# First-layer queries and keys as one 512-column group with weights moving, turned by VectorE; bias lines turned round; last product re-ordered

## Chip, cores and metric

The kernel runs on one core of one Trainium2 chip. The metric is the device time of one execution in microseconds, the median of three runs.

## What is computed

Two layers of a transformer on 256 tokens of width 2048, all in f32, and behind them a third layer with a convolution branch and windowed attention. The first layer, cut to what matters here:

```python
h = rmsnorm(x, attn_norm[0])
p = h @ even_w_in[0]                    # 2048 x 6144
qa, ka, va, qb, kb, vb = split(p)       # 1024 columns each
oa = chunked_relpos_attention(qa, ka, va, a_rel_bias)     # 8 heads of 128: branch A
ob = diff_attention(qb, kb, vb, t5_b, b_lambda, b_subln)  # 4 heads of 2 x 128: branch B
x = x + concatenate([oa, ob]) @ even_w_out[0]
x = x + (silu(h2 @ w_gate) * (h2 @ w_up)) @ w_down
```

The bias of A and B depends only on the distance of query and key. The second layer attends over selected tokens with latent keys and values, and has the same kind of output product and feed-forward part. The third layer ends in the product with `w_out_2`, a residual sum and a layer norm.

## The kernel before

Every weight is streamed once from HBM in units of 512 KB: SP issues a unit's DMA into `raw` (four slots), ScalarE rounds it to fp32r (`hi`, line 197), VectorE forms the rest (`lo`, line 203) into `ws` (four slots), and TensorE multiplies high and low parts of weights and activations. A unit's slot in `ws` is written again for the unit four further on, so `hi` of unit u + 4 waits for TensorE to be done with unit u (`s_mm`), and `lo` waits for `hi`; the DMA four units ahead again waits for `lo`.

Units are grouped (`Seg`): a group accumulates in two PSUM banks, and groups alternate between banks 0, 1 and 2, 3. There are two forms of multiplication. In `mul_T` (lines 227 to 230) the weights are stationary and the activations `hs` move, so the result comes with its columns in the partitions: a group of 256 columns has four units, and it is what scores need. In `mul_W` (line 251) activations are stationary and 512 weight columns move, twelve matmuls a unit, eight units a group; the result has tokens in the partitions. Before, phase A (`gA`) has ten groups, `QKVQKQKVQK`, where Q and K are of the first form and V of the second; phase B (`gBs`) has `QKVQKQKQKV`. Each phase has 48 units. A group of the first form is emptied by ScalarE (`crossing`, line 377) and VectorE (`scaled_drain`, lines 384 to 391, which writes the queries back to front in blocks), a V group by VectorE (line 1074).

The attention of a head pair is put between the units by hooks. TensorE's hook j of a group runs behind its unit j. `group_side` gives ScalarE and VectorE the hooks j behind `hi` or `lo` of unit j + 4, and an "early" hook stands ahead of it. The steps of a pair: scores `S_` (TensorE, lines 824, 825), `max_` (VectorE, line 839), `exps` (ScalarE, line 850), `soft` (VectorE, line 860, for B lines 927 to 935), the transposes `T_` (TensorE, line 867), `pt_` (ScalarE, line 878), the product with the values `V_` (TensorE, lines 887, 888), `out_hi`, `out_lo`; in B besides the norm of the output: `b_sq`, `b_st`, `b_a`, `rstd_act`, `b_on`, `b_hi`, `b_lo`. GpSimd (`stage`) brings the bias of a pair from DRAM, where two tables of lines (`lineA`, `lineB`) were written, each line read with a shift of one per partition, and copies it to `biasM` (line 1093).

`residual` is the output product with the residual sum. VectorE turns its result in 32x32 blocks (`turn_block`, line 585: 16 stream transposes a group) for the next product. `conv_*`, `gate_silu` and `late_out` finish the third layer's branches inside the last product (`so_run`), whose tables `so_act` and `so_dve` give ScalarE's and VectorE's work by unit.

Of the kernel before, what the change touches and what calls it, by code (L numbers as in the profile page):

```python
# [68 lines left out]
def build(nc, a):  # L69
# [228 lines left out]
    gA = Seg(1, [4, 4, 8, 4, 4, 4, 4, 8, 4, 4], [0, 2] * 5)  # L298
    gBs = Seg(1, [4, 4, 8, 4, 4, 4, 4, 4, 4, 8], [0, 2] * 5)
# [1809 lines left out]
```

## Time and profile before

| | |
|---|---|
| median of three runs | 2485.19 us (2485.16 to 2485.97) |
| profiled execution | 2484.79 us |
| its span, first to last instruction | 2483.0 us |
| TensorE busy | 2459.4 us (99%), mean granted clock 0.997 |
| VectorE busy | 1694.9 us (68%) |
| ScalarE busy | 1195.4 us (48%) |
| GpSimd busy | 52.8 us (2%) |
| DMA | 463.17 MB, 187 GB/s |

In the rows PE is TensorE's matmuls, PEld its weight loads, DVE VectorE, ACT ScalarE, POOL GpSimd. L251 is line 251 of the kernel. Times are us from the start of the span. A matmul's shown duration reaches into the next one, so the distance of two starts is what one costs. An idle time in brackets names the instruction that ended it.

### The profile page before, as it was taken

How to read it: one execution, taken by the hardware profiler on the slowest of the kernel's cores; microseconds unless marked ns; L12 is line 12 of the kernel's file. 1: busy time of each engine (PE TensorE's matmuls, PEld its weight loads, DVE VectorE, ACT ScalarE, POOL GpSimd, SP SyncE). 2: the span in 40 equal slices, each digit the busy share in tenths (PEclk: the TensorE clock that was granted, in tenths of full speed). 3: DMA queues.
4: the chain of work that ended last, by engine and by line, in shares of the span. 5: the costliest groups of instructions: out<-in, count | busy, mean ns of one | idle time of the engine just before them, and what ended most of it. 6: DMA issues, size and time to landing. Idle time of an engine off the chain costs nothing.

```text
span 2483.0 us, 32501 instructions
## 1 busy us (share of the span) xinstructions
PE 2459.4 (99%) x11622; PEld 2053.0 (83%) x11622; DVE 1694.9 (68%) x2538; ACT 1195.4 (48%) x1570; POOL 52.8 (2%) x72
## 2 busy tenths in 40 slices
PE   9999999999999999999999999999999999999997
PEld 8888888888888888888888888888888888888776
DVE  6556676666666666567867666666666656888985
ACT  5444455444444444445554544444444444546773
POOL 1000000000000000000220000000000000100000
PEclk9999999999999999999999999999999999999998
DMA  7555556666666655557545666666665555765453
GB/s 235 177 179 174 175 172 196 194 191 191 196 191 193 194 195 194 192 168 216 165 144 169 195 194 190 192 196 192 194 193 195 192 193 193 223 184 162 146 192 131
DMA packets 283278, 463.17 MB, mean 187 GB/s; under 512 B 17343, under 2 KB 99441, under 8 KB 282666
## 3 DMA queue, kind: packets, MB, share of 16 engines
q1 hardware_dynamic: 280768, 453.63, 59.5%
q0 software_dynamic: 1792, 8.11, 1.0%
q8 instruction: 63, 1.03, 0.2%
q14 instruction: 37, 0.30, 0.0%
q10 hardware_dynamic: 618, 0.09, 0.0%
HBM read 459.63 MB, written 2.14 MB: 186 GB/s over the span
## 4 chain that ended last, share of the span: by engine, by line
PE 95%; DVE 3%; ACT 1%; issue 1%; DMA 0%; DVEq 0%; ACTq 0%
PE PG L251 78%; PE PG L228 8%; PE PG L227 4%; DVE ws L203 1%; PE PS L824 1%; ACT ws L197 1%; PE PS L867 1%; PE PO L887 0%; PE PG L1280 0%; PE PG L240 0%; PE PO L1289 0%; DVE cacc L1505 0%; PE PS L825 0%; PE PG L230 0%; PE PO L888 0%
## 5 line engine op out<-in xcount | busy, mean ns | idle before, releaser
L203 DVE TENSOR_TENSOR ws<-raw,ws 128x1024 fp32r<-128x1024 f32 x860 | 1055.9, 1229 | 705.9 <-ACT ws L197 699.7
L197 ACT ACTIVATE ws<-raw 128x1024 fp32r<-128x1024 f32 x860 | 909.2, 1059 | 1073.6 <-PE PG L251 924.0
L251 PE MATMUL PG<-ws,hs 128*128 128x512 f32 x5568 | 1275.3, 390 | 0.3 <-DVE ws L203 0.3
L251 PEld LDWEIGHTS PG<-ws,hs 128*128 128x128 f32 x5568 | 1042.1, 188 | 216.6 <-issue 0.4
L251 PE MATMUL PG<-ws,fs 128*128 128x512 f32 x2112 | 479.0, 389 | 0.0
L251 PEld LDWEIGHTS PG<-ws,fs 128*128 128x128 f32 x2112 | 396.4, 188 | 82.3
L228 PE MATMUL PG<-hs,ws 128*128 128x512 f32 x880 | 308.3, 394 | 0.0
L251 PE MATMUL PG<-ws,os 128*128 128x512 f32 x1152 | 265.5, 391 | 2.7 <-DVE ws L203 2.7
L251 PEld LDWEIGHTS PG<-ws,os 128*128 128x128 f32 x1152 | 215.3, 188 | 48.6 <-DVE ws L203 4.2
L227 PE MATMUL PG<-hs,ws 128*128 128x256 f32 x825 | 235.1, 285 | 0.1
L228 PEld LDWEIGHTS PG<-hs,ws 128*128 128x128 f32 x880 | 163.7, 188 | 34.6 <-DVEq L1325 0.3
L585 DVE STREAM_TRANSPOSE turnb<-qst 32x256 f32<-32x256 f32 x352 | 153.4, 436 | 7.2
L227 PEld LDWEIGHTS PG<-hs,ws 128*128 128x128 f32 x825 | 155.7, 189 | 1.9 <-issue 0.4
L1505 DVE SCALAR_TENSOR_TENSOR cacc<-hc,convw,cacc 128x256 f32<-128x256 f32 x232 | 97.9, 478 | 0.0
L585 DVE STREAM_TRANSPOSE turnb<-x 32x256 f32<-32x256 f32 x192 | 83.6, 436 | 3.5
L850 ACT ACTIVATE ts<-ts,small 128x256 f32<-128x256 f32 x96 | 42.4, 443 | 25.4 <-DVE small L842 25.2
L790 ACT ACTIVATE cross<-PG,small 128x512 f32<-128x512 f32 x44 | 27.8, 685 | 33.2 <-PE PG L251 33.2
L803 DVE SCALAR_TENSOR_TENSOR qst<-PG,small,cross 128x512 f32<-128x512 f32 x44 | 31.0, 747 | 10.5 <-PE PG L251 10.5
L377 ACT ACTIVATE cross<-PG 128x512 f32<-128x512 f32 (+1 forms) x28 | 16.4, 587 | 39.8 <-PE PG L228 39.8
L384 DVE TENSOR_TENSOR cross<-PG,cross 128x512 f32<-128x512 f32 (+1 forms) x28 | 19.0, 679 | 18.5 <-ACT cross L377 18.4
L767 ACT ACTIVATE fs<-turnb 128x1024 f32 (+1 forms) x22 | 23.3, 1061 | 15.2 <-DVE turnb L585 15.2
L554 ACT ACTIVATE cross<-x 128x512 f32<-128x512 f32 x40 | 25.3, 632 | 11.2 <-DVE x L738 9.2
(287 smaller groups left out, 912.7 us busy)
## 6 DMA issues: line engine op xcount, KB each, us to landing
raw<-in_w_gate SPq DMA_DIRECT2D x176, 512.0 KB, 4.0
raw<-in_w_up SPq DMA_DIRECT2D x176, 512.0 KB, 4.3
raw<-in_w_down SPq DMA_DIRECT2D x176, 512.0 KB, 3.6
raw<-in_even_w_in SPq DMA_DIRECT2D x96, 512.0 KB, 4.0
raw<-in_w_in SPq DMA_DIRECT2D x52, 512.0 KB, 3.7
raw<-in_odd_w_in SPq DMA_DIRECT2D x44, 512.0 KB, 3.7
raw<-in_even_w_out SPq DMA_DIRECT2D x32, 512.0 KB, 4.3
raw<-in_odd_w_out SPq DMA_DIRECT2D x32, 512.0 KB, 3.6
```

The source lines that it names most:

```text
L197: e.activation(ws[j % RING][:, :, 0, :], raw[:, j % RING], ACT.Copy).then_inc(s_hi, 1)
L203: e.tensor_tensor(w[:, :, 1, :], raw[:, j % RING], w[:, :, 0, :].bitcast(F32), ALU.subtract).then_inc(s_lo, 1)
L227: e.matmul(PG[:, bank + c, 0:S], wl, rhs[:, k0 + kk, 0, :], start=False, stop=False)
L228: ins = e.matmul(PG[:, bank + c, :], wh, both, start=st, stop=end)
L251: ins = e.matmul(out[:, b, :], x_, w[:, kk, :, h, :], start=first and kk == 0 and n == 0, stop=last and kk == 1 and n == 2)
L554: e.activation(junk, xr[:, b, 512 * g:512 * (g + 1)], ACT.Square, accum_out=ss[:, b, g:g + 1]).then_inc(sem(p + "sq"), 1)
L585: return e.transpose(blocks_out, blocks_in)
L790: ins = e.activation(sil[:, b], gates[:, b, :], ACT.Silu, scale=rnT[:, b:b + 1])
L803: ins = e.scalar_tensor_tensor(nat_f[:, b], ups[:, b, :], rnT[:, b:b + 1], sil[:, b], ALU.mult, ALU.mult)
L824: e.matmul(PS[:, h, 0:S], q(h)[:, P:S], k(h), start=True, stop=True)
L850: e.activation(ts[:, h, src], ts[:, h, src], ACT.Exp, bias=nmx[:, n:n + 1], accum_out=sm[:, n:n + 1]).then_inc(sem(p + "e"), 1)
L1505: e.scalar_tensor_tensor(dst, hc[:, n, c:c + S], convw[:, n, c:c + 1], dst, ALU.mult, ALU.add).then_inc(sem("cv"), 1)
```

## The change

- **Queries and keys.** A group X now holds 256 query and the 256 key columns that belong to them, as a unit of two k-tiles by 512 columns (`pair_cols`, two DMAs of 256 KB), multiplied by `mul_W`. The phases are `XVXXVX` and `XVXXXV`, six groups of eight units each. ScalarE empties every group, scaled by a column, for X into `natqk`; `turn_pair` turns it on VectorE into `qk`, 16 stream transposes a pair. `pair_steps` hooks these by four behind units 0 to 3 of the group after X, the scores behind unit 4, the maxima early at unit 5, the softmax behind unit 6, transposes and values behind units 0 and 2 of the group after that. The spreading of the norm's factor over a tile and the drains on VectorE fall away in the first layer.
- **Start.** DMAs of x's last two quarters come behind four weight units; the transposes of the second quarter come behind unit 0; part of the dummy transposes fall away.
- **Bias lines.** The lines are written in the other direction, so queries and the scores' transposes are no longer turned round; instead GpSimd reads the bias back to front. The index scores and masks of the second layer follow.
- **Odd output product.** Transposes and values of the last head pair come one unit later.
- **Last product.** ScalarE's and VectorE's work at units 3 to 6 is ordered anew.

Its core:

```diff
+    natqk = at("natqk", [P, 2, 2, 512], F32, o1 + 24576)
+    qk = at("qk", [P, 2, 4, S], F32, o1 + 32768)
...
-        halved = min((u - gCv.ub) // RING + 1, gCv.U // RING) if isinstance(u, int) and u >= gCv.ub else 0
+        halved = sum(v % RING == j % RING and v <= (u if isinstance(u, int) else gEO.ub) for v in in_two)
...
-    gA = Seg(1, [4, 4, 8, 4, 4, 4, 4, 8, 4, 4], [0, 2] * 5)
-    gBs = Seg(1, [4, 4, 8, 4, 4, 4, 4, 4, 4, 8], [0, 2] * 5)
+    gA = Seg(1, [8] * 6, [0, 2] * 3)
+    gBs = Seg(1, [8] * 6, [0, 2] * 3)
...
+    order_of = {"A": "XVXXVX", "B": "XVXXXV"}
+    in_two = [sg.ub + 8 * g + j for sg, p in ((gA, "A"), (gBs, "B")) for g, kind in enumerate(order_of[p]) if kind == "X" for j in range(8)]
+    in_two += [gCv.ub + j for j in range(gCv.U)]
...
+    def pair_cols(W, j, c0):
+
+        return [W.rearrange("(t p) n -> p t n", p=P)[:, 2 * j:2 * j + 2, c:c + UC] for c in (c0, c0 + 1024)]
...
     def setup_sp(e):
         for c in range(4):
-            x_load(e, c)
-            load(e, gA, 0, c, cols(a["even_w_in"][0], c, 0))
+            if c < 2:
+                x_load(e, c)
+            load(e, gA, 0, c, pair_cols(a["even_w_in"][0], c, 0), 2)
+        x_load(e, 2)
+        x_load(e, 3)
...
-        src = bass.AP(tensor=lines.tensor, offset=h0 * LINE, ap=[[1, P], [LINE, n], [1, S]])
+        src = bass.AP(tensor=lines.tensor, offset=h0 * LINE + 1, ap=[[1, P], [LINE, n], [1, S]])
...
         lo(e, 0, 0)
         slice_lo(e, 0)
         lo(e, 1, 1)
+        lo(e, 2, 2)
         slice_lo(e, 1)
-        lo(e, 2, 2)
-        slice_lo(e, 2)
         lo(e, 3, 3)
-        slice_lo(e, 3)
         lines_first(e)
...
+    def back_to_front(t):
+
+        n = t.shape[2]
+        v = t[:, :, n - 1:n]
+        return bass.AP(tensor=v.tensor, offset=v.offset, ap=[list(v.ap[0]), list(v.ap[1]), [-1, n]])
...
         slice_hi(e, 0)
         hi(e, 1, 1)
-        slice_hi(e, 1)
         hi(e, 2, 2)
         squares(e, "n0", 0)
-        slice_hi(e, 2)
+        slice_hi(e, 1)
         hi(e, 3, 3)
-        slice_hi(e, 3)
-        squares(e, "n0", 1)
...
         keep_busy(e, 7)
         x_pe(e, 0)
-        keep_busy(e, 8)
-        x_pe(e, 1)
         keep_busy(e, 10)
...
-    def flipped(e, p, j, heads=slice(0, 2), turned=True):
+    def flipped(e, p, j, heads=slice(0, 2)):
 
         w(e, p + "T", j + 1)
         w(e, p + "O", j)
-        src = PS[:, heads, 0:384]
-        if turned:
-            v, n = PS[:, heads.start:heads.start + 1, P - 1:P], heads.stop - heads.start
-            src = bass.AP(tensor=v.tensor, offset=v.offset, ap=[list(v.ap[0]), [512, n], [P, 3], [-1, P]])
-            e.activation(pT[:, heads, :].rearrange("p h (b s) -> p h b s", s=P), src, ACT.Copy).then_inc(sem(p + "pT"), 1)
-            return
-        e.activation(pT[:, heads, :], src, ACT.Copy).then_inc(sem(p + "pT"), 1)
+        e.activation(pT[:, heads, :], PS[:, heads, 0:384], ACT.Copy).then_inc(sem(p + "pT"), 1)
...
+        def root_scale(e):
+            e.tensor_scalar(column, rnT, SCALE ** 0.5, None, ALU.mult).then_inc(sem("rq"), 1)
+
+        def number(pp, j):
+            return 4 * (pp == "B") + j
+
+        def turn_pair(e, pp, j, part):
+
+            x = number(pp, j)
+            if part[0] == 0:
+                g = [n for n, kind in enumerate(order_of[pp]) if kind == "X"][j]
+                e.wait_ge(s_drain, (gA if pp == "A" else gBs).group(0, g) + 3)
+            for n in part:
+                r, c = 32 * (n // 4), 32 * (n % 4)
+                blocks_in = natqk[r:r + 32, x % 2].rearrange("p b (t c) -> p b t c", c=P)[:, :, :, c:c + 32]
+                blocks_out = qk[c:c + 32, x % 2].rearrange("p t (b s) -> p b t s", s=P)[:, :, :, r:r + 32]
+                ins = e.transpose(blocks_out, blocks_in)
+            if part[-1] == 15:
+                ins.then_inc(sem("qkT"), 1)
 
         def S_(e, pp, j):
-            sg = gA if pp == "A" else gBs
-            scores(e, pp, j, lambda h: qst[:, 0, h, :], lambda h: kst[:, h, :],
-                   lambda: e.wait_ge(s_drain, sg.group(0, at_k[pp][j]) + 3))
+            x = number(pp, j)
+            scores(e, pp, j, lambda h, b: qk[:, x % 2, h, b * P:(b + 1) * P], lambda h: qk[:, x % 2, 2 + h, :], lambda: e.wait_ge(sem("qkT"), x + 1))
...
+                "pe": {0: {0: lambda e: x_pe(e, 1), 1: lambda e: (x_pe(e, 2), tables_pe(e)), 3: lambda e: x_pe(e, 3)}, 1: {1: lam_pe}},
+                "act": {0: {0: lambda e: squares(e, "n0", 1), 1: lambda e: slice_hi(e, 2), 2: lambda e: squares(e, "n0", 2), 3: lambda e: slice_hi(e, 3),
+                            4: lambda e: squares(e, "n0", 3), 5: lambda e: norm_act(e, "n0")}, 1: {2: lam_act}},
+                "dve": {0: {1: lambda e: slice_lo(e, 2), 2: lines_second, 3: lambda e: slice_lo(e, 3), 4: lambda e: norm_first(e, "n0"), 5: lambda e: (norm_second(e, "n0"), root_scale(e))},
+                        1: {3: lam_dve}}}[name].items()}
...
+        def put(at, g, u, d, f, early=False):
+
+            g, u = g + (u + d) // 8, (u + d) % 8
+            u = ("early", u) if early else u
+            at[g, u] = (lambda f0=at[g, u]: (f0(), f())) if (g, u) in at else f
+
+        def pair_steps(name, e, at, pp, j, g):
+
+            if name == "pe":
+                put(at, g, 4, 0, lambda: S_(e, pp, j))
+                if number(pp, j) < 7:
+                    put(at, g, 4, 4, lambda: T_(e, pp, j))
+                if number(pp, j) < 6:
+                    put(at, g, 4, 6, lambda: V_(e, pp, j))
+            elif name == "act":
+                put(at, g, 4, 1, lambda: exps(e, pp, j))
+                if number(pp, j) < 7:
+                    put(at, g, 4, 4, lambda: pt_(e, pp, j))
+                if pp == "A":
+                    put(at, g, 4, 7, lambda: out_hi(e, pp, j, 2 * j))
+            else:
+                for n in range(4):
+                    put(at, g, n, 0, lambda n=n: turn_pair(e, pp, j, range(4 * n, 4 * n + 4)))
+                put(at, g, 4, 1, lambda: max_(e, pp, j), early=True)
+                put(at, g, 4, 2, lambda: soft(e, pp, j))
+                if pp == "A":
+                    put(at, g, 4, 7, lambda: out_lo(e, pp, j, 2 * j))
+
+        def norm_steps(name, e, at, j, g):
+
+            if name == "pe":
+                put(at, g, 4, 0, lambda: b_st(e, j))
+            elif name == "act":
+                put(at, g, 2, 0, lambda: b_sq(e, j))
+                put(at, g, 5, 0, lambda: rstd_act(e, "B", j))
+                put(at, g, 7, 0, lambda: b_hi(e, j))
+            else:
+                put(at, g, 5, 0, lambda: b_a(e, j), early=True)
+                put(at, g, 6, 0, lambda: b_on(e, j))
+                put(at, g, 7, 0, lambda: b_lo(e, j))
...
+                for g, v in start_hooks(name, e).items():
+                    at.update({(g, j): f for j, f in v.items()})
+                for j, g in enumerate((1, 3, 4)):
+                    pair_steps(name, e, at, "A", j, g)
...
+            pair_steps(name, e, at, "A", 3, 0)
+            norm_steps(name, e, at, 0, 2)
+            norm_steps(name, e, at, 1, 4)
+            for j, g in enumerate((1, 3, 4, 5)):
+                pair_steps(name, e, at, "B", j, g)
...
+                        group_pe(e, seg, 0, g, W_mul(hs), hk, (lambda j: w(e, "n0lo", 2 * j + 2)) if first and not is_b else None)
                     elif name == "act":
-                        def cross_over(_):
-                            if kind != "V":
-                                if not is_b:
-                                    w(e, "n0sq", 8)
-                                crossing(e, seg, 0, g)
-                        group_side(e, seg, 0, g, hi, cross_over, hk)
+                        def drain(_):
+                            e.wait_ge(s_mm, seg.end(0, g) + RING)
+                            pairs_seen = number(p, order_of[p][:g].count("X"))
+                            if kind == "X":
+                                e.wait_ge(sem("rq"), 1)
+                                w(e, "qkT", pairs_seen - 1)
+                            for b in (0, 1):
+                                out = natqk[:, pairs_seen % 2, b, :] if kind == "X" else vab[:, order_of[p][:g].count("V"), b, :]
+                                ins = e.activation(out, PG[:, seg.banks[g] + b, :], ACT.Copy, scale=(column if kind == "X" else rnT)[:, b:b + 1])
+                            ins.then_inc(s_drain, 1)
+                        group_side(e, seg, 0, g, hi, drain, hk)
...
-                e.tensor_copy(biasM[:, 0:n, 0:S], biasE[:, h:h + n, :]).then_inc(sem(p + "bm"), 1)
+                e.tensor_copy(biasM[:, 0:n, 0:S], back_to_front(biasE[:, h:h + n, :])).then_inc(sem(p + "bm"), 1)
...
-             {0: lambda e: (c_S(e, 7, 1), c_V(e, 6, 0)), 2: lambda e: flips(e, "C", 7), 3: lambda e: c_V(e, 7, 1)},
-             {0: lambda e: out_hi(e, "C", 6, 12), ("early", 1): lambda e: exps(e, "C", 7), 2: lambda e: flipped(e, "C", 7), 3: lambda e: out_hi(e, "C", 7, 14)},
-             {0: lambda e: c_max(e, 7), 1: lambda e: out_lo(e, "C", 6, 12), ("early", 2): lambda e: norms(e, "C", 7), ("early", 4): lambda e: out_lo(e, "C", 7, 14)})
+             {0: lambda e: (c_S(e, 7, 1), c_V(e, 6, 0)), 3: lambda e: flips(e, "C", 7), 4: lambda e: c_V(e, 7, 1)},
+             {0: lambda e: out_hi(e, "C", 6, 12), ("early", 1): lambda e: exps(e, "C", 7), 3: lambda e: flipped(e, "C", 7), 4: lambda e: out_hi(e, "C", 7, 14)},
+             {0: lambda e: c_max(e, 7), 1: lambda e: out_lo(e, "C", 6, 12), ("early", 2): lambda e: norms(e, "C", 7), ("early", 5): lambda e: out_lo(e, "C", 7, 14)})
...
         rstd_act(e, "L")
         e.preload_act_table(ACT.Silu)
-        conv_silu(e, 0)
-        conv_silu(e, 1)
...
-              4: lambda e: (conv_hi(e, 0), conv_hi(e, 1), late_out(e, 9, 1), conv_silu(e, 2)),
-              5: lambda e: (gate_silu(e, slice(4, 8), 20), conv_silu(e, 3)), 6: lambda e: conv_hi(e, 2), 7: lambda e: conv_hi(e, 3),
+              4: lambda e: (conv_silu(e, 0), conv_hi(e, 0), conv_silu(e, 1)),
+              5: lambda e: (conv_hi(e, 1), late_out(e, 9, 1), gate_silu(e, slice(4, 8), 20), conv_silu(e, 2)),
+              6: lambda e: (conv_silu(e, 3), conv_hi(e, 2)), 7: lambda e: conv_hi(e, 3),
...
-    so_dve = {0: first_dve, 2: lambda e: (spread_dve(e), conv_scale(e, 0), conv_scale(e, 1)),
-              3: lambda e: (centre_conv(e, 1), conv_gate(e, 0), conv_gate(e, 1), conv_lo(e, 0)),
-              4: lambda e: (conv_lo(e, 1), conv_scale(e, 2), conv_scale(e, 3)),
+    so_dve = {0: first_dve, 2: lambda e: (spread_dve(e), conv_scale(e, 0)),
+              3: lambda e: (conv_gate(e, 0), conv_scale(e, 1), conv_lo(e, 0)), 4: lambda e: conv_gate(e, 1),
+              5: lambda e: (conv_lo(e, 1), centre_conv(e, 1), conv_scale(e, 2), conv_scale(e, 3)),
               6: lambda e: (conv_gate(e, 2), conv_gate(e, 3), conv_lo(e, 2)), 7: lambda e: conv_lo(e, 3)}
```

## Rows read from the trace of the kernel before

**Rows 1.** The page's fourth part: shares of the chain that ended last, by engine.

```profile
PE 95%; DVE 3%; ACT 1%; issue 1%; DMA 0%; DVEq 0%; ACTq 0%
```

**Rows 2.** Waits of PE, whole span: us in total, times, longest.

```profile
PE PG L251 <- DVE ws L203: 3.0, 4, 1.6
```

**Rows 3.** Timeline of PE: start, us, line, operation, count, idle before and its releaser.

```profile
37.22 3.00 PE L251 MATMUL PG<-ws,hs 128*128 128x512 f32 x12 [0.30 <-DVE ws L203]
...
1302.08 5.70 PE L251 MATMUL PG<-ws,os 128*128 128x512 f32 x24
...
1309.33 0.88 PE L867 MATMUL PS<-ident,ts 128*128 128x128 f32 x6 [1.55 <-DVE ts L860]
...
2386.52 11.17 PE L251 MATMUL PG<-ws,os 128*128 128x512 f32 x48
...
2402.93 5.90 PE L251 MATMUL PG<-ws,os 128*128 128x512 f32 x24 [1.58 <-DVE ws L203]
...
2409.29 15.98 PE L251 MATMUL PG<-ws,os 128*128 128x512 f32 x69 [0.46 <-DVE ws L203]
```

**Rows 4.** Chain that ended last, in order of time: start, us, what.

```profile
9.45 0.87 PE PG L613 x8
...
33.60 0.45 PE PO L706 x2
...
73.68 0.46 PE PG L228 x2
...
84.97 0.46 PE PG L228 x2
...
116.23 0.43 PE PS L824 x2
...
117.53 10.94 PE PG L251 x48
...
128.47 0.66 PE PS L867 x6
...
220.71 0.46 PE PG L228 x2
...
231.82 0.46 PE PG L228 x2
```

**Rows 5.** Timeline of DVE in phase A, a low part behind a free slot.

```profile
121.50 1.23 DVE L203 TENSOR_TENSOR ws<-raw,ws 128x1024 fp32r<-128x1024 f32 x1 [1.53 <-ACT ws L197]
```

**Rows 6.** Timeline of DVE in the even output product: low parts and turning quarters.

```profile
335.63 1.23 DVE L203 TENSOR_TENSOR ws<-raw,ws 128x1024 fp32r<-128x1024 f32 x1 [1.50 <-ACT ws L197]
...
336.77 1.78 DVE L585 STREAM_TRANSPOSE turnb<-x 32x256 f32<-32x256 f32 x4
...
338.56 1.23 DVE L203 TENSOR_TENSOR ws<-raw,ws 128x1024 fp32r<-128x1024 f32 x1
...
339.82 1.78 DVE L585 STREAM_TRANSPOSE turnb<-x 32x256 f32<-32x256 f32 x4
```

**Rows 7.** Timeline of DVE in phase B: norm, output, softmax and what follows each.

```profile
226.06 0.42 DVE L655 TENSOR_TENSOR nt<-na,ny 128x256 f32<-128x256 f32 x1
...
228.37 1.22 DVE L203 TENSOR_TENSOR ws<-raw,ws 128x1024 fp32r<-128x1024 f32 x1
...
231.61 0.88 DVE L989 SCALAR_TENSOR_TENSOR os<-qst,small,os 128x256 fp32r<-128x256 f32 x2
...
244.06 0.17 DVE L927 RECIPROCAL small<-small 128x4 f32<-128x4 f32 x1
...
245.72 0.68 DVE L384 TENSOR_TENSOR cross<-PG,cross 128x512 f32<-128x512 f32 x1
```

**Rows 8.** Timeline of DVE in the last product: two scalings of 128x512.

```profile
2391.58 1.29 DVE L1879 TENSOR_TENSOR cacc<-cacc,ny 128x512 f32<-128x512 f32 x2
```

**Rows 9.** Timeline of POOL: first copy of the bias.

```profile
35.93 1.62 POOL L1093 COPY biasM<-biasE 128x512 f32<-128x512 f32 x1
```

**Rows 10.** Windows: stretch, length, each engine's busy us (count), clock, DMA share, GB/s.

```profile
2400.00:2405.00 5.00, 3.42 (x15) 2.50 (x15) 1.78 (x3) 4.50 (x7) 0.00 (x0) 1.00 0.41 138
```

More of the change, by code:

```diff
@@ L215, in load, with mul_T @@
         e.dma_start(dst, src).then_inc(s_raw[j % RING], 16)
-    def mul_T(e, bank, j, k0, rhs, first, last, tiles=(0, 1), ready=lambda kk: None):
+    def mul_T(e, bank, j, k0, rhs, first, last, tiles=(0, 1)):
         w = ws[j % RING]
         for kk in range(UK):
-            ready(kk)
             for c in tiles:
@@ L377, in crossing, with scaled_drain @@
         e.activation(cross[:, q // 2, 0:m], PG[:, q:q + m, S:2 * S], ACT.Copy).then_inc(s_cross, 1)
-    def scaled_drain(e, seg, i, k, dst, crossed, n, scale=1.0, turned=None):
+    def scaled_drain(e, seg, i, k, dst, crossed, n, scale=1.0):
         m, q = dst.shape[1], seg.banks[k]
@@ L385, in scaled_drain @@
         e.wait_ge(sem("summed"), n + 1)
-        if turned is None:
-            return e.scalar_tensor_tensor(dst, c, scale, bc(rn, m), ALU.mult, ALU.mult)
-        if turned:
-            e.scalar_tensor_tensor(dst[0:turned], c[0:turned], scale, bc(rn, m)[0:turned], ALU.mult, ALU.mult)
-        t = slice(turned, P)
-        return e.scalar_tensor_tensor(backward(dst[t]), blocks(c[t]), scale, blocks(bc(rn, m)[t]), ALU.mult, ALU.mult)
+        return e.scalar_tensor_tensor(dst, c, scale, bc(rn, m), ALU.mult, ALU.mult)
     QT = D // 4
@@ L1020, in out @@
-            def out(pp, j, g, u):
-                put(e, at, {"pe": {}, "act": {(g, u): lambda: out_hi(e, pp, j, 2 * j)}, "dve": {(g, u): lambda: out_lo(e, pp, j, 2 * j)}}[name])
-            if not is_b:
-                for k, v in start_hooks(name, e).items():
-                    put(e, at, {(k, j): f for j, f in v.items()})
-                broad("A", 0, 2)
-                out("A", 0, 3, 2)
-                narrow("A", 1, 5)
-                out("A", 1, 6, 3)
-                broad("A", 2, 7)
-                out("A", 2, 8, 2)
-                return at
@@ L1052, in f @@
                     hk = {j: f_ for (g_, j), f_ in at.items() if g_ == g}
-                    n = order_of[p][:g].count("Q") + order_of[p][:g].count("K")
                     if name == "pe":
-                        mul = W_mul(hs) if kind == "V" else T_mul(hs)
-                        if first and not is_b:
-                            mul = lambda e, bank, jj, j, f_, l_: mul_T(e, bank, jj, UK * j, hs, f_, l_, ready=lambda kk: w(e, "n0lo", 4 * j + kk + 1))
-                        group_pe(e, seg, 0, g, mul, hk)
+                        group_pe(e, seg, 0, g, W_mul(hs), hk, (lambda j: w(e, "n0lo", 2 * j + 2)) if first and not is_b else None)
@@ L1100, in weights @@
                 n = order_of[p][:g].count(kind)
-                for j in range(seg.groups[g]):
+                for j in range(8):
                     if kind == "V":
-                        load(e, seg, 0, seg.first(g) + j, wide_cols(W, j, c0 + 2048 + 2 * UC * n), 1)
-                    elif is_b or g:
-                        load(e, seg, 0, seg.first(g) + j, cols(W, j, c0 + 1024 * (kind == "K") + UC * n))
+                        load(e, seg, 0, 8 * g + j, wide_cols(W, j, c0 + 2048 + 2 * UC * n), 1)
+                    elif is_b or g or j > 3:
+                        load(e, seg, 0, 8 * g + j, pair_cols(W, j, c0 + UC * n), 2)
         phase(sp=weights, pe=run("pe"), act=run("act"), dve=run("dve"), pool=stage)
@@ L1335, in c_S @@
     def c_S(e, j, par):
-        scores(e, "C", j, lambda h: qst[:, par, h, :], lambda h: kC[:, bass.ds(2 * j + h, 1), :][:, 0, :],
+        scores(e, "C", j, lambda h, b: qst[:, par, h, b * P:(b + 1) * P], lambda h: kC[:, bass.ds(2 * j + h, 1), :][:, 0, :],
                lambda: e.wait_ge(s_drain, gQ.gb + j + 3))
@@ L1362, in c_pool @@
         prepare(1, 1)
-        def body(i, *_):
-            prepare(2 * i, 0)
-            prepare(2 * i + 1, 1)
-        with e.Fori(1, 4) as i:
-            body(i)
+        for j in range(2, 8):
+            prepare(j, j % 2)
     def c_hooks(name, e, j, par):
@@ L1794, in act @@
                     n, j = n0 + 2 * g + half, 4 * half
-                    hk["early", j] = lambda n=n: n == 0 or flipped(e, "D", n - 1, turned=False)
+                    hk["early", j] = lambda n=n: n == 0 or flipped(e, "D", n - 1)
                     hk[j] = lambda j=j: start_at(e, name_of, g, j)
@@ L1900, in first_act @@
     def first_act(e):
-        flipped(e, "D", 7, turned=False)
+        flipped(e, "D", 7)
         gate_silu(e, slice(12, 16), 16)
```

86 lines of the change are left out of this document (19 added, 67 removed).

## The prediction

> **What bounds the kernel now.** I read the chain that ended last first: TensorE is 95% of it [rows 1], so in nearly every stage only what delays or shortens TensorE's own queue counts. Then the waits of that queue [rows 2]: behind the set-up it waits for VectorE's low parts four times, 3.0 us in all. Its timeline [rows 3] places them: 0.30 us at 37.22, 1.55 at 1309.33 in the odd output product (for the softmax), the rest from 2398 to 2409 in the last product. In the first layer's projections, 37 to 305 us, it waits for nothing. VectorE and ScalarE have slack there, and what the change gives them costs time only where TensorE comes to wait for it.
>
> **Measures for the sums.** A unit is one 512 KB weight tile. In the form with weights moving (12 matmuls of 512 columns) four units take 10.94 us, 2.735 each (at 117.53) [rows 4]. In the form with weights stationary a group of four units takes 11.29 us (73.68 to 84.97) or 11.11 (220.71 to 231.82), mean 2.80 a unit [rows 4]. A block of scores takes 1.30 us (116.23 to 117.53), the six transposes of the weights 0.66 [rows 4].
>
> **Queries and keys in one group.** After the first eight units, phases A and B have 24 + 32 = 56 units of the stationary form. They turn into the moving form: 56 x (2.80 - 2.735) = 3.6 us less; by the two rows 2.4 to 4.9. The scores, transposes and value products are as many as before.
>
> **The turning, which I think decides.** The result of such a group has the sequence in its partitions and must be turned: 16 stream transposes a pair, eight pairs. `pair_steps` hooks four of them behind VectorE's low parts of units 0, 1, 2 and 3 of the next group, and puts the scores into TensorE's queue behind unit 4, with a wait for the sixteenth. The added wait stands in TensorE's queue, so units 5 to 7 and all that follows wait with it. How late is the sixteenth? A low part's slot comes free only when TensorE is done with the unit. The unit that ends at 117.53 + 2.735 = 120.265 [rows 4] has its low part start at 121.50 [rows 5]: 1.235 us behind the unit's end. VectorE then goes on to the next thing 1.14 us later, four transposes of just this shape hold it 1.79, and from a low part queued directly behind them to the next four are 1.26 [rows 6]. So, from the end of unit 0: first four done at 1.235 + 1.14 + 1.79 = 4.17. Each further quarter takes 1.26 + 1.79 = 3.05, more than TensorE's 2.735, so VectorE is not held up by units any more: 7.22, 10.27, 13.32. There the scores can start. TensorE comes to them at 4 x 2.735 = 10.94. Wait: 2.38 us. Were VectorE caught up before the last quarter, it would still be 4.17 - 2.735 = 1.43, since the last quarter is hooked only one unit ahead of its user.
>
> Pair by pair: A0, A1, A3 and B1 are of this clean kind: 4 x 2.38 = 9.5 (A0 has three small lambda instructions ahead of its last quarter, which I leave to the range). In A2's and B0's group TensorE also does the last pair's transposes (0.66) and values (1.30, as the scores) between units 0 and 4, which delays TensorE by 1.96; VectorE, held to unit 3 again, then does `out_lo` (0.65, one 128x512 instruction as in [rows 8]) and the last quarter. Same count: 2.13 each, 4.3. At B2 transposes of one head (0.33), values and the sum of squares (0.86, four matmuls as the two of 0.43 at 116.23) precede the scores, and the wait shrinks to 0.6. At B3 VectorE comes with a debt: in B2's group unit 6 has `b_on` (2.31 us, 226.06 to 228.37) and `soft` (1.66, 244.06 to 245.72), unit 7 `b_lo` (0.88) [rows 7]. The softmax is ready 0.9 us after TensorE asks for it, and the turning starts at 16.36 instead of 2.38 on a clock in which its unit 0 ends at 12.25; the same steps end 2.8 us behind TensorE. Together 9.5 + 4.3 + 0.6 + 0.9 + 2.8 = 18.1 us. Bounds: 11.5 (each of eight at 1.43) and 25 (each as B3, with A0's three and more debt).
>
> The Trainium skill speaks against this move: VectorE: DVE Perf Modes, The three transpose paths and Rules for kernel authors, send a 128x128 transpose to TensorE where PSUM may hold it, since VectorE turns 32x32 blocks only. Its figure for VectorE's 128x128, 311 ns for bf16, would make an estimate of 0.62 us for a quarter here, and the waits would shrink to about 0.3 us each; no run shows that pace, the rows above show 1.79.
>
> **Drains.** ScalarE empties both kinds of group now (two 128x512 reads ahead of one high part, 1.3 us if they take what VectorE's two take [rows 8]), VectorE none. ScalarE's high part of that unit comes later by that, the low part too, and its user is three units, 8.2 us, behind: nothing while that cover stands; gone, it would be 1.3 us a group. Two DMAs for one on SP's queue go the same way: their data is asked for four units ahead. Both at nothing.
>
> **Set-up.** The first group's eight units get 8 x (11.11/4 - 2.735) = 0.3 us shorter, the spread product (0.45, at 33.60) goes, and the 0.30 wait at 37.22 [rows 3, 4]; against that the transposes of x's second quarter (0.87, at 9.45) [rows 4], until now done while TensorE had to wait anyway, come behind unit 0, and unit 0 needs a second tile's low part, 0.4 later (two of that kind take 0.88 [rows 7]). Sum 0.2; I take 0, range -0.5 to +1.5. Dummy transposes fall away ahead of unit 0, so TensorE is idle there for a while.
>
> **Bias lines turned round.** GpSimd copies the bias back to front now. The first copy ends at 37.55 [rows 9] and is needed behind unit 4 of the second group, at about 37.2 + 5 x 2.735 = 51; later ones have a whole pair. Even at twice its 1.62 us it is hidden. Without that cover it would hold the maxima, and through them the softmax. The scores, transposed reads and selection in the odd layer only lose or exchange a negative stride; the plain and the turned forms of the drain bound that at nothing. Zero, range 0 to 1.
>
> **Odd output product.** The last transposes move from behind unit 2 to behind unit 3. From 1302.08 to 1309.33 two units take 7.25 where 5.47 are work [rows 3]: 1.8 us go, as the weights were 1.55 late and a unit is 2.735. The values follow one unit later and their low part is needed two units after; nothing is late next. Range 1.5 to 1.8.
>
> **Last product.** Unit 4 starts at 2386.52, unit 11 at 2409.29 [rows 3]: 22.77 us for 19.15 of work, 3.6 lost. The new order lets the low part of unit 8 go ahead of most of the gating. Worked out from 2391.58 [rows 8] in queue order, with ScalarE's work at the lengths it has in this stage (a pair of Silus 1.05, a 128x512 copy 0.6, a high part 1.0): scale 0 and low part 7 to 2393.3, gate 0 behind the first Silu to 2394.1, scale 1, first output part, then low part 8 done at 2396.6, before TensorE wants it (2386.52 + 10.94 = 2397.46). Low part 9 ends at 2398.4. But high part 10 stands behind the third Silu, which waits for the centring and scaling on VectorE: low part 10 ends at 2404.2, against 2402.93: 1.3 late. Low part 11, behind `conv_hi` 2, ends at 2407.7 against 2407.0: 0.75. Unit 11 starts at 2407.75: 1.5 us gained, range 0 to 3.6.
>
> **Sum** against the profiled execution, 2484.79 us (span 2483.0 and 1.8 around it): 2484.8 - 3.6 + 18.1 + 0 - 1.8 - 1.5 = 2496.0. The median of the runs shown is 0.4 above that execution: 2496.4 us. The forecast's own range: all terms at their friendly ends 2485.2 - 4.9 + 11.5 - 0.5 - 1.8 - 3.6 = 2485.9, at the others 2485.2 - 2.4 + 25 + 1.5 + 1 - 1.5 - 0 = 2508.8; since they hardly all fall together, 2488 to 2504.
>
> **Rivals.** *No wait at the scores.* If the turning is through before unit 4 ends, by a faster transpose or because I misplace a hook, what is left is 2485.2 - 3.6 - 1.8 - 1.5 = 2478.3, faster. It decides from the point where a quarter takes under about 0.35 us from the last low part on; every row at 1.79 speaks against it, that all four quarters are named ahead of unit 4 speaks for it. Chance 0.11. The figure of the Trainium skill's page VectorE: DVE Perf Modes would leave 8 x 0.26 = 2.1 us of waits, 2480.4, of which I hold 0.01 of that chance. *The waits are there, but short* (1.5 or less each, VectorE never in debt): 8 x 1.5 or less on 2478.3 gives 2480 to 2490. The rows' 3.05 against 2.735 speaks against it. Chance 0.10. *The clock.* Nine waits of 2.4 us could let TensorE's clock fall from 2.4 to 1.2 GHz. The row of 2400 to 2405 holds the 1.58 us gap and shows a granted clock of 1.00 [rows 10]; no longer gap inside the work is there to judge by. A fall that lasts one unit costs 2.7 us: with each of nine, 25 us, about 2521. Chance 0.05. The Trainium skill's page TensorE: Matmul & The Clock Gate, HAM oscillation, has idle gaps between bursts put a kernel back to the low clock each time. *ScalarE or the streams late*: the drain ahead of the high part and the debts add up past the 8.2 us of cover at some groups, 1.3 us each, 12 groups: up to 2512. Chance 0.04.
>
> **Chances.** Forecast 0.70. A run tells about 0.2%, 5 us, from no change: faster (below 2480.2) is the first rival, 0.11; same takes the short waits and a little of the forecast's low end, 0.12; slower 0.77. The range leaves out the first rival and the clock: 2484 to 2505.
>
> **What would show it.** In the profile after: TensorE's waits list, at its top, the scores' line held by VectorE's transposes, eight times, 1.5 to 3 us each, the shortest at B2; phase A + B about 15 us longer though matmuls of the large form take 0.228 us apart throughout; the wait at 1309 gone; two waits of about 1 us in place of three in the last product. Wrong it is if the scores start directly behind unit 4, if a quarter of the turning takes other than 1.8 us, or if the granted clock leaves 1.00.

## The result and the profile after

| | before | after |
|---|---|---|
| median | 2485.58 us (2485.16 to 2486.67, 4 runs) | 2507.16 us (2506.87 to 2507.44, 4 runs) |
| ratio | | 1.0086, 95% interval 1.0069 to 1.0104 |
| profiled execution, its span | 2484.79, 2483.0 us | 2507.44, 2505.6 us |

The change makes the kernel 21.6 us slower. The forecast was 11.2 us slower (2496.4, range 2484 to 2505): the right sign, about half the size, and the result lies outside the range.

First the waits of TensorE in the kernel after (engine, line, what it waited for: us in total, times, longest). They answer to [rows 2].

```profile
PE PS L815 <- DVE qk L910: 17.7, 8, 2.8
...
PE PG L252 <- DVE ws L205: 1.8, 2, 1.4
PE PS L858 <- DVE ts L938: 1.7, 1, 1.7
...
PE PG L252 <- DVE hs L561: 0.8, 1, 0.8
```

The scores (L815) wait eight times for the turning (L910), where [rows 2] had no wait of this kind. The transposes of B2 (L858) wait once for the softmax. A0 to A3 are the head pairs of branch A, B0 to B3 those of branch B. TensorE's timeline of after gives each wait its place (start, us, what, idle before and its releaser), in the order A0, A1, A2, A3, B0, B1, B2 (scores, then transposes), B3:

```profile
53.50 0.70 PE L815 MATMUL PS<-qk 128*128 128x256 f32 x2 [2.54 <-DVE qk L910]
...
104.75 0.70 PE L815 MATMUL PS<-qk 128*128 128x256 f32 x2 [2.46 <-DVE qk L910]
...
133.94 0.70 PE L815 MATMUL PS<-qk 128*128 128x256 f32 x2 [2.18 <-DVE qk L910]
...
183.58 0.70 PE L815 MATMUL PS<-qk 128*128 128x256 f32 x2 [2.46 <-DVE qk L910]
...
212.80 0.70 PE L815 MATMUL PS<-qk 128*128 128x256 f32 x2 [2.17 <-DVE qk L910]
...
263.32 1.22 PE L815 MATMUL PS<-qk 128*128 128x256 f32 x2 [2.76 <-DVE qk L910]
...
291.43 0.70 PE L815 MATMUL PS<-qk 128*128 128x256 f32 x2 [0.71 <-DVE qk L910]
...
305.65 0.55 PE L858 MATMUL PS<-ident,ts 128*128 128x128 f32 x3 [1.73 <-DVE ts L938]
...
319.57 0.70 PE L815 MATMUL PS<-qk 128*128 128x256 f32 x2 [2.46 <-DVE qk L910]
```

Together 19.5 us. In the row of 263.32 the same two matmuls take 1.22 us and not 0.70: they run at half the clock. Windows of after show the granted clock, as a share of 2.4 GHz (stretch, length, busy us of PE, PEld, DVE, ACT, POOL with counts, then the clock, DMA share and GB/s). The reader is to look at the number behind POOL:

```profile
54.00:58.00 4.00, 4.00 (x14) 3.29 (x14) 2.12 (x11) 0.00 (x0) 1.14 (x2) 0.58 0.46 143
104.00:110.00 6.00, 5.25 (x18) 4.39 (x19) 3.32 (x13) 0.00 (x0) 1.26 (x2) 0.72 0.58 177
134.00:138.00 4.00, 4.00 (x20) 3.44 (x21) 2.56 (x11) 0.00 (x0) 0.95 (x2) 1.00 0.45 152
184.00:188.00 4.00, 4.00 (x15) 3.27 (x14) 2.22 (x11) 0.00 (x0) 0.60 (x3) 0.57 0.62 199
212.00:216.00 4.00, 3.20 (x16) 2.80 (x17) 3.37 (x13) 0.00 (x0) 0.15 (x1) 1.00 0.50 156
262.00:268.00 6.00, 4.68 (x16) 3.98 (x17) 3.88 (x14) 0.00 (x0) 0.22 (x1) 0.72 0.55 175
306.00:310.00 4.00, 4.00 (x20) 3.30 (x19) 3.96 (x8) 1.44 (x2) 0.00 (x0) 1.00 0.43 135
318.00:326.00 8.00, 6.43 (x23) 5.33 (x24) 4.11 (x15) 0.68 (x2) 0.00 (x0) 0.79 0.44 140
```

Behind A0, A1, A3, B1 and B3 TensorE's clock went from 2.4 to 1.2 GHz and came back; this is called a fall below. Behind A2, B0 and the wait of B2's transposes it stayed. What a fall takes is the length of a window times one minus its clock: 4 x 0.42, 6 x 0.28, 4 x 0.43, 6 x 0.28 and 8 x 0.21, about 1.7 us each, 8.5 together. The row of before that answers is [rows 10], with 1.00.

Phases A and B go from 267.8 us (37.22 to 305.01) to 293.8 (36.96 to 330.78): 26.0 more. The forecast for the moving form was 3.6 less; the listed waits are 19.5 and the clock 8.5, which leaves 1.6. Most of that is in the waits themselves, since the list counts idle time from the end that is shown, and a matmul's shown duration reaches past what it costs. For A1:

```profile
99.64 2.65 PE L252 MATMUL PG<-ws,hs 128*128 128x512 f32 x11
104.75 0.70 PE L815 MATMUL PS<-qk 128*128 128x256 f32 x2 [2.46 <-DVE qk L910]
```

Eleven matmuls at 0.228 end at 102.15 and not at 102.29, so the wait is 2.60 and not 2.46. Counted like this the nine waits are 20.9 us together, and 25.8 of the 26.0 have a place, if the 3.6 are right.

### The profile page after: what moved, and what is told of

Read it like the earlier page. It is cut to its first block, busy times and chain, and to the rows that moved or that the text cites. A ratio compares the mean times of both kernels' runs of the same rounds, so it can differ in the third digit from the quotient of the medians.

```text
span 2505.6 us, 32089 instructions
## 1 busy us (share of the span) xinstructions
PE 2464.0 (98%) x11356; PEld 2045.3 (82%) x11356; DVE 1723.3 (69%) x2623; ACT 1202.1 (48%) x1578; POOL 51.7 (2%) x72
## 4 chain that ended last, share of the span: by engine, by line
PE 81%; DVE 4%; ACT 1%; issue 1%; DVEq 0%; ACTq 0%
PE PG L252 74%; PE PG L229 3%; PE PG L228 1%; DVE ws L205 1%; PE PG L241 0%; ACT ws L199 0%; DVE cacc L1508 0%; PE PG L1286 0%; PE PS L858 0%; PE PO L872 0%; PE PS L815 0%; DVE pT L1179 0%; PE PO L1295 0%; DVE x L2059 0%; ACT ts L1709 0%
## 5 line engine op out<-in xcount | busy, mean ns | idle before, releaser
L252 PE MATMUL PG<-ws,hs 128*128 128x512 f32 x6336 | 1459.8, 391 | 0.8 <-DVE hs L561 0.8
L252 PEld LDWEIGHTS PG<-ws,hs 128*128 128x128 f32 x6336 | 1189.4, 188 | 247.8 <-issue 1.0
L229 PE MATMUL PG<-hs,ws 128*128 128x512 f32 x368 | 129.0, 394 | 0.0
L228 PE MATMUL PG<-hs,ws 128*128 128x256 f32 x345 | 98.9, 287 | 0.2 <-DVE hs L561 0.2
L229 PEld LDWEIGHTS PG<-hs,ws 128*128 128x128 f32 x368 | 68.4, 188 | 14.2 <-DVEq L1331 0.3
L228 PEld LDWEIGHTS PG<-hs,ws 128*128 128x128 f32 x345 | 65.1, 189 | 1.2 <-issue 0.4
L910 DVE STREAM_TRANSPOSE qk<-natqk 32x256 f32<-32x256 f32 x128 | 55.8, 436 | 2.1
L547 ACT ACTIVATE cross<-x 128x512 f32<-128x512 f32 x40 | 25.3, 632 | 11.2 <-DVE x L729 9.2
L815 PE MATMUL PS<-qk 128*128 128x256 f32 x32 | 12.0, 462 | 17.7 <-DVE qk L910 17.7
```

Of the source, the lines that this page charges most:

```text
L228: e.matmul(PG[:, bank + c, 0:S], wl, rhs[:, k0 + kk, 0, :], start=False, stop=False)
L229: ins = e.matmul(PG[:, bank + c, :], wh, both, start=st, stop=end)
L252: ins = e.matmul(out[:, b, :], x_, w[:, kk, :, h, :], start=first and kk == 0 and n == 0, stop=last and kk == 1 and n == 2)
L547: e.activation(junk, xr[:, b, 512 * g:512 * (g + 1)], ACT.Square, accum_out=ss[:, b, g:g + 1]).then_inc(sem(p + "sq"), 1)
L910: ins = e.transpose(blocks_out, blocks_in)
```

## Experiments

Two theories. *Theory 1*: the order of the hooks makes the waits, since VectorE's quarter takes longer than TensorE's unit, and some waits let the clock fall. *Theory 2*: something else in the new form (ScalarE's drains, two DMAs a tile, the set-up, VectorE's debts) costs the missing 10.8 us.

**The scores one unit later.** A pair's whole chain moves, from S_ to out_lo, the norm's steps too; the turning stays.

```
-                put(at, g, 4, 0, lambda: S_(e, pp, j))
+                put(at, g, 5, 0, lambda: S_(e, pp, j))
...
-                put(at, g, 6, 0, lambda: b_on(e, j))
+                put(at, g, 6, 1, lambda: b_on(e, j))
```

> The kernel after, with the scores and all that hangs on them (maxima, exponentials, softmax, transposes, values, norms) one unit later, behind unit 5 of a group instead of unit 4; the turning stays where it is. Theory 1 (the order of hooks makes the waits, and the waits make the clock fall): VectorE is through with the turning 13.3 us behind unit 0, TensorE comes at 13.7, so at least six of the eight waits go, B3 may keep up to 1.5; no granted clock under 1.00 between 37 and 305 us; phases A and B take 264 to 268 us instead of 293.9, the kernel 2507.2 - 29 + (0 to 3) = 2478 to 2481. Theory 2 (something else in the new form costs most of it: ScalarE's drains, two DMAs a tile, the form itself): only the listed waits of 17.7 us go, 2489 or more, and other waits or longer units appear.

Measured: 2487.96 us, ratio 1.0009 (0.9999 to 1.0018). 19.2 us go, not 26 to 29. Seven of the eight waits at the scores are gone. Three waits are left in TensorE's timeline:

```profile
247.41 0.70 PE L815 MATMUL PS<-qk 128*128 128x256 f32 x2 [2.34 <-DVE qk L910]
...
288.48 0.90 PE L858 MATMUL PS<-ident,ts 128*128 128x128 f32 x3 [2.87 <-DVE ts L938]
...
334.74 5.46 PE L252 MATMUL PG<-ws,os 128*128 128x512 f32 x23 [1.28 <-DVE os L992]
```

and the clock falls behind the second, for longer than in any wait of after (10 us at 0.66, 3.4 us lost):

```profile
286.00:296.00 10.00, 7.52 (x22) 6.08 (x23) 9.11 (x21) 3.40 (x5) 0.00 (x0) 0.66 0.44 143
```

2478.3 (the sum without waits) + 2.34 + 2.87 + 1.28 + 3.4 = 2488.2. The expectation of 2478 to 2481 missed, I think, because I moved the norm's steps as well: b_lo came ahead of B1's first quarter, and b_on ahead of B2's softmax; the next run tests it. That speaks for theory 1, but with several things moved at once it isn't a proof.

**The same, with the norm's steps left in their place.** The edit is shown against the kernel just before. Of the norm only the squares stay one unit later; the softmax now goes ahead of the norm's scaling, and in the output product the last pair's norm is scaled a unit earlier than in the kernel just before.

```
-                put(at, g, 6, 1, lambda: b_on(e, j))
+                put(at, g, 6, 0, lambda: b_on(e, j))
...
-            norm_steps(name, e, at, 0, 2)
-            norm_steps(name, e, at, 1, 4)
             for j, g in enumerate((1, 3, 4, 5)):
                 pair_steps(name, e, at, "B", j, g)
+            norm_steps(name, e, at, 0, 2)
+            norm_steps(name, e, at, 1, 4)
```

> As the kernel with the scores a unit later (2487.96), but the steps of the norm (reciprocal root, scaling, low part of heads 8 on) go back to the units where the kernel after has them, only the squares stay one later, the softmax goes ahead of them at unit 7, and the last norm in the output product is scaled a unit earlier. In that kernel's trace these late steps are what holds the rest: 2.34 us at B1's scores, 2.87 at B2's transposes, with a fall of the clock behind it, 1.28 in the output product. Theory 1 (what is left above 2478.3 is these three and the fall): 2.6 + 3.1 + 1.7 + 1.5 = 8.9 us go, 2479 to 2481, faster than before (2485.6) by about 0.2%. Theory 2 (the moving form or the set-up cost something not seen as a wait): 2483 or more, with clock 1.00 and no waits.

Measured: 2479.87 us (2479.57 to 2481.90, 11 runs), ratio 0.9979 (0.9970 to 0.9988), faster than both kernels. One wait is left at the scores, B3's, and the window of phases A and B has a full clock:

```profile
PE PS L815 <- DVE qk L910: 1.3, 1, 1.3
```

```profile
36.00:305.00 269.00, 267.65 (x1224) 221.68 (x1223) 191.16 (x358) 130.93 (x199) 9.51 (x22) 1.00 0.57 180
```

2478.3 + 1.3 = 2479.6 against 2479.87. With waits and falls gone, everything else in the change comes to the sum that the prediction had put down, so theory 2 falls: nothing near 10 us is left for it. That the two agree to 0.3 us is in part luck. The interval of the ratio is about 2 us to each side, and in this trace the second group starts at 36.65, 0.6 us earlier than before where 0 was put down, while phases A and B (to 303.07) are 1.4 us shorter, or 2.9 without the wait, where 3.6 was put down.

**The waits filled with work.** Dummy transposes ahead of the scores in five pairs; the scores start when they did.

```
         x = number(pp, j)
+        w(e, pp + "pT", j)
+        for _ in range((22, 22, 0, 22, 0, 22, 0, 22)[x]):
+            e.transpose(PS[:, 0, 384:512], ident[:], ident[:])
```

> The kernel after, with 22 dummy transposes (0.11 us each, 2.4 us) in TensorE's queue ahead of the wait at the scores of A0, A1, A3, B1 and B3, the five behind which the granted clock was 0.67 to 0.83. TensorE comes to the scores at the same time, but has worked until then. Theory 1 (these five waits let the clock fall, 1.7 us lost each): clock 1.00 in 53 to 60, 104 to 110, 183 to 190, 263 to 268, 320 to 330; scores of these pairs 0.70 us for the first two matmuls and not 1.22; the kernel 2507.2 - 8.3 = about 2499. Theory 2 (the clock is no part of the missing 10 us, VectorE's debts are): no change, 2507, or up to 2 us more where a dummy ends behind the sixteenth transpose.

Measured: 2500.07 us, ratio 1.0056 (1.0040 to 1.0073): 7.1 us less for work that nobody reads. The five falls are gone, as expected. A new one came at B0, whose wait is what it was (2.18 us):

```profile
206.00:212.00 6.00, 4.52 (x15) 3.76 (x16) 4.02 (x15) 0.45 (x1) 0.85 (x2) 0.72 0.58 178
```

Five falls less and one more are four: 1.8 us each by the medians, against 1.7 from the windows; in the two traces the stretch from behind the second group's second unit to the output product is 6.2 us shorter, 1.6 each. TensorE comes to the scores when it did and only isn't idle until then, so this shows the clock's share directly.

**Shorter idle times.** The same edit with 4 and with 8 dummies.

> As the one before, but with only four dummy transposes (0.44 us) ahead of each of the same five waits: the idle time is 2.46 - 0.44 = about 2.0 us in each, shorter than the 2.17 and 2.18 behind which the clock stayed. Theory 1 with a bound between 2.18 and 2.46 us of idle time: clock 1.00 throughout, about 2499. Theory 1 with a cost that grows with the length of the wait: a small part of the 8.3 us, 2505 to 2507. Theory 2 (not the gap's length but the pair decides): clock falls as before, 2507.

Measured: 2503.59 us, ratio 1.0070 (1.0053 to 1.0087). None of the three expectations is met. The waits that were 2.46 to 2.76 are now 2.00 to 2.32; the clock still falls in A0, A1 and A3, and doesn't in B1 and B3. Timeline and window of A3, then of B1:

```profile
183.97 0.81 PE L815 MATMUL PS<-qk 128*128 128x256 f32 x2 [2.00 <-DVE qk L910]
...
263.71 0.70 PE L815 MATMUL PS<-qk 128*128 128x256 f32 x2 [2.32 <-DVE qk L910]
```

```profile
184.00:188.00 4.00, 4.00 (x13) 3.38 (x14) 2.43 (x11) 0.00 (x0) 0.00 (x0) 0.57 0.64 215
...
262.00:268.00 6.00, 4.29 (x21) 3.69 (x22) 4.25 (x15) 0.11 (x1) 0.88 (x2) 1.00 0.56 175
```

A wait of 2.00 let it fall and one of 2.32 did not. So in the one execution traced, length alone doesn't decide between 2.0 and 2.5 us.

> The kernel after with eight dummy transposes (0.88 us) ahead of the scores of A0, A1, A3, B1 and B3. With four, waits of 2.00 to 2.10 us still let the clock fall in A0, A1 and A3, but not 2.32 and 2.02 in B1 and B3. Now the waits are about 1.6 us. If the idle time's length decides together with something else, no clock falls at this length, 2500 as with 22. If the place alone decides (A0, A1, A3 fall whatever the length, so long as there is a wait), the clock falls at these three and the time is 2503 to 2505.

Measured: 2501.43 us, ratio 1.0066 (1.0051 to 1.0081). A0, A1, A3, B1 and B3 now wait 1.57 to 1.87 us and none falls. The place alone is refuted. One fall is left, at B0 again, behind a wait of the length that left the clock alone in after (2.17):

```profile
207.88 1.07 PE L815 MATMUL PS<-qk 128*128 128x256 f32 x2 [2.18 <-DVE qk L910]
```

**The same waits at other moments.** Twelve dummy transposes behind unit 6 of the first group were to make every wait come 1.3 us later.

```
-                "pe": {0: {0: lambda e: x_pe(e, 1), 1: lambda e: (x_pe(e, 2), tables_pe(e)), 3: lambda e: x_pe(e, 3)}, 1: {1: lam_pe}},
+                "pe": {0: {0: lambda e: x_pe(e, 1), 1: lambda e: (x_pe(e, 2), tables_pe(e)), 3: lambda e: x_pe(e, 3), 6: lambda e: keep_busy(e, 12)}, 1: {1: lam_pe}},
```

> The kernel after with 12 dummy transposes (1.3 us of work) behind unit 6 of the first group: every wait behind it is as long as before and comes 1.3 us later. If the place of a wait within some rhythm of the chip decides which of them lets the clock fall, other pairs than A0, A1, A3, B1 and B3 show a granted clock under 1.00. If the length decides (2.46 and more fall, 2.18 and less not), the same five. The time: 2507.2 + 1.3 = 2508.5 for the same five, up to 1.7 us less or more for each fall that goes or comes.

Measured: 2506.81 us, ratio 1.0084 (1.0069 to 1.0100). The waits are as long as before to 0.01 us, the falls are not the same: A1, A3, B0 and B1. Windows of A0, B0 and B3 in this kernel, then the scores of A1 and B0:

```profile
54.00:58.00 4.00, 3.04 (x16) 2.63 (x17) 3.37 (x14) 0.00 (x0) 0.00 (x0) 1.00 0.52 165
...
212.00:218.00 6.00, 5.40 (x19) 4.49 (x20) 3.17 (x13) 0.00 (x0) 0.88 (x2) 0.72 0.51 158
...
320.00:326.00 6.00, 4.78 (x23) 4.10 (x24) 3.77 (x14) 0.35 (x1) 0.00 (x0) 1.00 0.53 174
```

```profile
104.61 1.14 PE L815 MATMUL PS<-qk 128*128 128x256 f32 x2 [2.46 <-DVE qk L910]
...
212.60 0.70 PE L815 MATMUL PS<-qk 128*128 128x256 f32 x2 [2.17 <-DVE qk L910]
```

A0 (2.54) and B3 (2.46) keep their clock, B0 (2.17) loses it. So a wait's length doesn't settle whether the clock falls. What does stays open. The shift was not what I had meant it to be: A0 comes 1.5 us later, but without its fall the scores of A1, A2, A3 and B0 start 0.1 to 0.2 us earlier in the span than in after (104.61 against 104.75, 212.60 against 212.80). And one execution of each kernel was traced: the four executions of this one took 2504.18 to 2508.62 us, those of after 2506.87 to 2507.44, so which waits have a fall may differ from one execution to the next as well. No run separates the moment from such chance.

**Twelve of sixteen transposes.** A quarter of the queries' and keys' blocks is left out from the third pair on.

```
-            for n in part:
+            for n in (part if x < 2 else list(part)[:3]):
```

> The kernel after, with 12 instead of 16 transposes of the turning from the third pair on (three of each quarter; a quarter of the queries' and keys' blocks of six pairs is left out). A quarter takes 1.34 instead of 1.78 us. Theory 1 (VectorE's pace decides, 3.05 us a quarter with its low part against TensorE's 2.735): the pace falls to 2.6, VectorE is held to units again, the waits of A2, A3, B0, B1 and B3 shrink to about 1.0 each and the clock stays; A0 and A1 keep 2.5 and their falls: 2507.2 - 8.5 of waits - 3 x 1.7 of clock = about 2494. Theory 2 (the turning waits for ScalarE's drain, or the scores for something else): 2505 or more.

Measured: 2497.05 us, ratio 1.0046 (1.0029 to 1.0063); about 2494 was expected. A0 and A1 are as they were, falls too. A3, B1 and B3 wait 1.12 (about 1.0 was expected), A2 and B0 1.72, and the clock falls nowhere else. A3's wait shrinks by 1.34 us for a last quarter that is 0.45 shorter: the rest is the debt of the quarters before. A quarter with its low part was longer than a unit and now isn't, and VectorE is idle again behind A3's first quarter, until ScalarE's high part lets the next low part start:

```profile
173.87 1.23 DVE L205 TENSOR_TENSOR ws<-raw,ws 128x1024 fp32r<-128x1024 f32 x1 [0.25 <-ACT ws L199]
```

In A2 and B0, where VectorE is held to a unit before the last quarter, only 0.46 goes. I had put these two at 1.0 as well and left out that out_lo stands ahead of the last quarter there; that and B2's 1.73, which stays, is most of the 3 us missed.

**The two small parts alone**, in the kernel before: the last transposes and values of the odd output product one unit later, and the new order of the gating.

```
-             {0: lambda e: (c_S(e, 7, 1), c_V(e, 6, 0)), 2: lambda e: flips(e, "C", 7), 3: lambda e: c_V(e, 7, 1)},
+             {0: lambda e: (c_S(e, 7, 1), c_V(e, 6, 0)), 3: lambda e: flips(e, "C", 7), 4: lambda e: c_V(e, 7, 1)},
...
-              3: lambda e: (centre_conv(e, 1), conv_gate(e, 0), conv_gate(e, 1), conv_lo(e, 0)),
+              3: lambda e: (conv_gate(e, 0), conv_scale(e, 1), conv_lo(e, 0)), 4: lambda e: conv_gate(e, 1),
```

> The kernel before with only the two small parts: the last transposes and values of the odd output product one unit later, and the gating of the last product re-ordered. By the terms of the prediction -1.8 and -1.5, by the trace of after -1.8 and -1.3: 2482.3 to 2482.6, ratio about 0.9987. Rival (their gains come back later, as the streams run no faster): no change, 2485.6.

Measured: 2482.28 us, ratio 0.9988 (0.9979 to 0.9997), 3.1 us less than before in the same series (2485.40): what was expected. The interval only just leaves out no change.

## Why the prediction was wrong in size and right in kind

**The waits: right in kind, 2.8 us too low in sum.** The rows of VectorE in A1's group show the steps as the prediction counted them, one low part with its quarter 3.05 us from the next:

```profile
92.61 1.22 DVE L205 TENSOR_TENSOR ws<-raw,ws 128x1024 fp32r<-128x1024 f32 x1 [0.40 <-ACT ws L199]
93.75 1.78 DVE L910 STREAM_TRANSPOSE qk<-natqk 32x256 f32<-32x256 f32 x4
95.54 1.22 DVE L205 TENSOR_TENSOR ws<-raw,ws 128x1024 fp32r<-128x1024 f32 x1
...
98.59 1.23 DVE L205 TENSOR_TENSOR ws<-raw,ws 128x1024 fp32r<-128x1024 f32 x1
...
101.64 1.23 DVE L205 TENSOR_TENSOR ws<-raw,ws 128x1024 fp32r<-128x1024 f32 x1
102.90 1.79 DVE L910 STREAM_TRANSPOSE qk<-natqk 32x256 f32<-32x256 f32 x4
```

| | forecast | listed |
|---|---|---|
| A0, A1, A3 | 2.38 each | 2.54, 2.46, 2.46 |
| A2, B0 | 2.13 each | 2.18, 2.17 |
| B1 | 2.38 | 2.76 |
| B2: scores, transposes | 0.6, 0.9 | 0.71, 1.73 |
| B3 | 2.8 | 2.46 |
| sum | 18.1 | 19.5 |

Against the list most are 0.04 to 0.16 too low; by the distances of starts the nine are 20.9 us, 2.8 more than forecast. B2's softmax is furthest off (0.9 against 1.73); a longer wait there leaves less of VectorE's debt for B3 (2.46 against 2.8), and the two together are 0.5 over. B1 was counted as a clean pair and isn't one: the norm's low part (L992) stands directly ahead of the low part that its first quarter follows.

```profile
250.40 0.88 DVE L992 SCALAR_TENSOR_TENSOR os<-qst,small,os 128x256 fp32r<-128x256 f32 x2
251.19 1.22 DVE L205 TENSOR_TENSOR ws<-raw,ws 128x1024 fp32r<-128x1024 f32 x1
252.32 1.77 DVE L910 STREAM_TRANSPOSE qk<-natqk 32x256 f32<-32x256 f32 x4
```

The row of [rows 6] at 1.78 held for the turning too. The Trainium skill's page VectorE: DVE Perf Modes, Rules for kernel authors, sends such a transpose to TensorE. Whether that would have been better here no run shows: with the scores one unit later VectorE's turning left one wait of 1.3 us. The 311 ns for bf16 that the Trainium skill's same page gives under The three transpose paths was not to be carried over: a quarter took 1.78 us here, not the 0.62 that the prediction's estimate made of it.

**The clock: this step failed.** The prediction put it down as a rival with a chance of 0.05, on the ground that the gap of 1.58 us in [rows 10] left the clock at 1.00. That row says nothing of a gap of 2.4, and the rival was worked out as all nine waits or none; the sum and the range had the clock at nothing. Five of nine let it fall, at 1.7 us and not 2.7, 8.5 us together. Without them the kernel would have been at about 2498.7, inside the range. Of the missing 10.8 us the clock is 8.5 and the longer waits are 2.8; that is 0.5 too much, of which the earlier start of the second group is 0.3. A cost that no row shows should have had its bounds in the range, here 0 to 9 x 2.7 us, and a range with them would have held 2507.2. The Trainium skill's TensorE: Matmul & The Clock Gate, HAM oscillation, tells of a kernel with DMA waits of about 3 to 5 us, where the clock is put back behind every one. The waits here are shorter, and the runs agree in kind only: it happened behind 17 of 29 waits between 2.0 and 2.9 us.

**The moving form, set-up, drains, two DMAs, bias: right as a sum, with some luck.** The kernel without the waits shows them together: 2482.28 (the small parts alone) less 3.6, plus its one wait of 1.3, is 2480.0 against 2479.87. As said there, the start gave 0.6 us and the phases 0.7 less than forecast, so two misses cancel. In after the second group starts at 36.96, 0.3 earlier than [rows 3] had it. None of these parts was run by itself.

**Odd output product: right.** In after the transposes start with no idle time before them, where [rows 3] had 1.55:

```profile
1327.80 8.43 PE L252 MATMUL PG<-ws,os 128*128 128x512 f32 x36
1336.06 0.82 PE L858 MATMUL PS<-ident,ts 128*128 128x128 f32 x6
1336.64 2.99 PE L252 MATMUL PG<-ws,os 128*128 128x512 f32 x12
```

**Last product: right to 0.2 us.** Unit 4 to unit 11 takes 2431.99 - 2410.53 = 21.46 us, 1.3 less than the 22.77 of [rows 3]; 1.5 was forecast. The two waits, forecast at 1.3 and 0.75:

```profile
2410.53 16.61 PE L252 MATMUL PG<-ws,os 128*128 128x512 f32 x72
2428.51 3.06 PE L252 MATMUL PG<-ws,os 128*128 128x512 f32 x12 [1.36 <-DVE ws L205]
2431.99 2.35 PE L252 MATMUL PG<-ws,os 128*128 128x512 f32 x9 [0.42 <-DVE ws L205]
```

## What to carry to other kernels

Where a side engine is given work in equal parts behind each unit of TensorE, compare part plus its standing work with the unit: here 3.05 against 2.735, so the debt grows with each part, and the user must stand where the last part is done (13.3 us behind unit 0, so behind unit 5) and not where it was ordered (behind unit 4). One place later, with the norm's steps kept where they were, turned 22 us lost into 5.5 gained; 3.1 of the 5.5 are the two small parts. A wait in TensorE's queue has a second price, the clock: behind waits of 2 us and more it fell in over half the cases here, at 1.7 us each beside the wait itself, so such a term belongs in the range unless a row with a gap as long shows otherwise. And of a chain that is moved, leave the steps of its neighbours where they are.

## What the runs showed of the hardware

- In the traces of the eight kernels here with new waits in phases A and B and at the output product behind them, 29 waits of TensorE were between 2.00 and 2.87 us, and the granted clock fell behind 17 of them; behind 25 between 0.26 and 1.87 us it never fell. The shortest with a fall was 2.00 (A3 with four dummies), the longest without one 2.54 (A0 with the waits moved). Many of these waits are the same one in another kernel, so the counts can't be read as chances.
- A fall cost 1.7 us by the windows and 1.6 to 1.8 by filling the waits; behind the wait of 2.87 it cost 3.4.
- Twelve dummy transposes ahead of all these waits left their lengths as they were, and other pairs showed a fall in the traced execution: out went A0 and B3, in came B0. The pairs in between came within 0.2 us of where they had been.
- Four f32 stream transposes of 32x256 took VectorE 1.77 to 1.79 us in every row of the turning shown here.
- Dummy transposes in TensorE's idle time were worth more than they cost: 22 ahead of each of five waits made the kernel 7.1 us faster.
